# The order of weight splits, input squares and latent transposes around three block boundaries of a two-block transformer kernel

## The reference

```
f = swiglu(rms_norm(x, g[0]), w_in, w_out);  x = x + 0.5 * rms_norm(f, g[1])
h = rms_norm(x, g[2]);  m = attention(h);    x = x + rms_norm(m, g[3])
f = swiglu(rms_norm(x, g[4]), w_in, w_out);  x = x + 0.5 * rms_norm(f, g[5])
rms_norm(x, g) = x / sqrt(mean(x*x) + 1e-6) * g
```

## Time and profile before

| | |
|---|---|
| median of 3 runs | 1407.59 us (1407.07 to 1408.98) |
| the profiled execution, its own time | 1407.68 us |
| its span, first to last instruction | 1406.4 us |
| PE busy | 1378.2 us, 98% of the span |
| DVE busy | 918.6 us, 65% |
| ACT busy | 763.0 us, 54% |
| transfers | 297.19 MB, 211 GB/s on the mean |
| mean granted clock of TensorE | 0.999 |

### The profile page before, as it was taken

One profiled execution on the slowest core, in us unless ns is written; L12 is line 12 of the kernel. 1 busy time (PEld: TensorE's weight loads), 2 busy tenths in 40 slices (PEclk: granted clock), 3 DMA queues, 4 the chain that ended last, 5 costly groups with the idle time before them and its releaser, 6 DMA issues.

```text
span 1406.4 us, 18962 instructions
## 1 busy us (share of the span) xinstructions
PE 1378.2 (98%) x7530; PEld 1159.4 (82%) x7530; DVE 918.6 (65%) x1310; ACT 763.0 (54%) x1107; POOL 37.1 (3%) x72
## 2 busy tenths in 40 slices
PE   6999999999999999999999999999999999999998
PEld 5888799878888788888997888888888888788886
DVE  3667866777864866657576766657666477766653
ACT  4535456465454655546685554546555387654542
POOL 0000100000000000000241000000000000000000
PEclk9999999999999999999999999999999999999999
DMA  9756545558886588866434688866888651378872
GB/s 385 269 209 233 211 141 180 183 190 292 289 250 202 195 239 246 239 215 197 166 121 150 203 242 241 238 203 206 236 244 237 197 186 63 126 222 245 239 231 89
DMA packets 142233, 297.19 MB, mean 211 GB/s; under 512 B 65856, under 2 KB 80192, under 8 KB 138560
## 3 DMA queue, kind: packets, MB, share of 16 engines
q1 hardware_dynamic: 140128, 290.08, 64.6%
q10 hardware_dynamic: 2016, 5.90, 1.3%
HBM read 280.47 MB, written 15.47 MB: 210 GB/s over the span
## 4 chain that ended last, share of the span: by engine, by line
PE 90%; DVE 5%; ACT 3%; DMA 1%; issue 1%; SPq 0%; POOL 0%; ACTq 0%
PE PS L742 25%; PE PS L758 14%; PE PS L760 14%; PE PS L759 14%; PE PS L396 5%; PE PS L397 4%; PE PS L398 4%; DVE WL L1656 1%; PE PS L430 1%; DMA MC<-in_mod 1%; PE PS L431 1%; PE PS L432 1%; PE PS L979 1%; ACT WH L1080 1%; PE PS L728 1%
## 5 line engine op out<-in xcount | busy, mean ns | idle before, releaser
L1656 DVE TENSOR_TENSOR WL<-RAW,WH 128x1024 fp32r<-128x1024 f32 (+1 forms) x440 | 532.3, 1219 | 262.8 <-ACT WH L1080 262.1
L1080 ACT ACTIVATE WH<-RAW 128x1024 fp32r<-128x1024 f32 (+1 forms) x440 | 458.3, 1057 | 273.9 <-DMA RAW<-in_up 132.9
L758 PE MATMUL PS<-WH,XH 128*128 128x512 f32 (+1 forms) x928 | 363.9, 392 | 3.4 <-DVE XL L2127 2.9
L760 PE MATMUL PS<-WH,XL 128*128 128x512 f32 (+1 forms) x928 | 361.5, 389 | 0.0
L759 PE MATMUL PS<-WL,XH 128*128 128x512 f32 (+1 forms) x928 | 361.3, 389 | 0.0
L758 PEld LDWEIGHTS PS<-WH,XH 128*128 128x128 f32 x928 | 174.3, 188 | 42.9 <-DVE XL L2127 6.6
L760 PEld LDWEIGHTS PS<-WH,XL 128*128 128x128 f32 x928 | 174.3, 188 | 36.0
L759 PEld LDWEIGHTS PS<-WL,XH 128*128 128x128 f32 x928 | 174.4, 188 | 34.9
L742 PE MATMUL PS<-WH,GH 128*128 128x512 f32 x440 | 136.4, 391 | 0.0
L742 PE MATMUL PS<-WL,GH 128*128 128x512 f32 x440 | 135.7, 390 | 0.0
L742 PE MATMUL PS<-WH,GL 128*128 128x512 f32 x440 | 135.7, 390 | 0.0
(11 more groups left out here) (355 smaller groups left out, 1745.1 us busy)
## 6 DMA issues: line engine op xcount, KB each, us to landing
RAW<-in_up SPq DMA_DIRECT2D x220, 512.0 KB, 4.4
RAW<-in_down SPq DMA_DIRECT2D x110, 512.0 KB, 4.3
RAW<-in_win SPq DMA_DIRECT2D x28, 512.0 KB, 4.7
laid<-BT SPq DMA_DIRECT2D x55, 256.0 KB, 4.9
RG<-laid SPq DMA_DIRECT2D x55, 256.0 KB, 4.9
MC<-in_mod SPq DMA_DIRECT2D x8, 1024.0 KB, 11.5
RAW<-in_mod SPq DMA_DIRECT2D x8, 1024.0 KB, 5.7
RAW<-in_sbqk SPq DMA_DIRECT2D x16, 512.0 KB, 4.8
```

The source lines that it names most:

```text
L758: e.matmul(o_[:, 0:n], l, w[:, s], start=(k == 0), stop=False, skip_group_check=True)
L760: m = e.matmul(o_[:, 0:n], ll, w[:, s], start=False, stop=(k == KD - 1), skip_group_check=True)
L1080: e.activation(WH[s][:, 0:c], RAW[s][:, 0:c], ACT.Copy).then_inc(*sig("hi", j))
L1656: e.tensor_tensor(WL[s][:, 0:c], RAW[s][:, 0:c], WH[s][:, 0:c].bitcast(F32), ALU.subtract).then_inc(*sig("lo", j))
```

## The change

It touches the order of calls only; no operation is added, removed or resized.

- ACT, b = 1 and b = 6, row block 1: the split of c0+6 and the square of x for row block 0 move behind the two `turned` calls of row block 1; the split of c0+5 stays ahead of them. At b = 6, row block 0, the split of c0+3 joins that of c0+2, and that of c0+4 moves ahead of the second half.
- ACT, b = 5: the splits of c0+5 and c0+6 leave the boundary. After it, c0+5 (`mlakv` 1) is split behind `latents_turned(0)`, and c0+6 and c0+7 (`mlaq` 0 and 1) behind `latents(1)` and the table load, ahead of `keys_kept(0, 0)`; c0+8 and c0+9 follow later.
- DVE, b = 1 and b = 6: both halves are scaled and the first is made low before the split of c0+5, and the reciprocal of `scale_of_input(b, 0)` stands behind the second half. At b = 6 the split of c0+4 moves behind `renewed`, and that of c0+3 ahead of the low part of row block 0's second half. At b = 5 the splits of c0+4 to c0+6 leave the chain: c0+4 is split at the boundary's end, c0+5 ahead of `latents(1)`, c0+6 behind it and ahead of `latents_gained(1)`, and c0+7 behind `latents_low(1)`.
- PE: `latents_turned(0)` is run at p = 7 and not at p = 6, that is behind `mla_step(2, 1)`.

```diff
--- before.py
+++ after.py
@@ -1019,7 +1019,7 @@
                 if p == 3:
                     turn(5, 1, 0)
                     turn(5, 1, 1)
-                if p == 6:
+                if p == 7:
                     latents_turned(0)
                 if p >= 4:
                     mla_step(p - 4, 1)
@@ -1379,10 +1379,10 @@
                 square_of(b, 0, 1)
                 root(b, 0)
                 if b == 6:
-                    split(c0 + 2)
+                    split(c0 + 3)
                     turned(b, 0, 0)
+                    split(c0 + 4)
                     turned(b, 0, 1)
-                    split(c0 + 4)
                 elif b < 7:
                     split(c0 + 4)
                     turned(b, 0, 0)
@@ -1393,13 +1393,24 @@
                     turned(b, 0, 1)
                 square_of(b, 1, 1)
                 root(b, 1)
-                if b < 7:
+                if b in (1, 6):
+                    split(c0 + 5)
+                    turned(b, 1, 0)
+                    turned(b, 1, 1)
+                    split(c0 + 6)
+                    scale_of_input(b, 0)
+                    scale_of_input(b, 1)
+                elif b == 5:
+                    scale_of_input(b, 0)
+                    turned(b, 1, 0)
+                    turned(b, 1, 1)
+                    between()
+                    scale_of_input(b, 1)
+                elif b < 7:
                     split(c0 + 6)
                     scale_of_input(b, 0)
                     turned(b, 1, 0)
                     turned(b, 1, 1)
-                    if b == 5:
-                        between()
                     scale_of_input(b, 1)
                 ac.wait_ge(*at("x", b, 1, 1))
                 for n in {1: (3, 4)}.get(b, (b + 3,)):
@@ -1606,10 +1617,11 @@
                 latents(0)
 
             boundary(5, chunk["mla", 0], first_latents)
-            split(chunk["mlaq", 2])
             latents_turned(0)
+            split(chunk["mlakv", 1])
             latents(1)
             e.preload_act_table_set("exp_and_others")
+            split(chunk["mlaq", 1])
             keys_kept(0, 0)
             latents_turned(1)
             keys_kept(0, 1)
@@ -2181,8 +2193,8 @@
                     scaled(b, 0, 0)
                     turned(b, 0, 0)
                     scaled(b, 0, 1)
+                    split(c0 + 3)
                     turned(b, 0, 1)
-                    split(c0 + 3)
                 elif 1 < b < 6:
                     split(c0 + 3)
                     scaled(b, 0, 0)
@@ -2198,32 +2210,45 @@
                     turned(b, 0, 1)
                 added(b, 1)
                 sum_of(b, 1)
-                if b < 7:
+                if b < 5:
                     split(c0 + 4)
                 inverse(b, 1)
                 renewed(b, 1, 0)
                 renewed(b, 1, 1)
+                if b == 6:
+                    split(c0 + 4)
                 if b < 7:
-                    if b < 2:
+                    if b in (1, 6):
+                        scaled(b, 1, 0)
+                        scaled(b, 1, 1)
+                        turned(b, 1, 0)
+                        split(c0 + 5)
+                        turned(b, 1, 1)
+                        scale_of_input(b, 0)
+                    elif b == 5:
+                        scale_of_input(b, 0)
+                        scale_of_latents(0)
+                        scaled(b, 1, 0)
+                        scaled(b, 1, 1)
+                        turned(b, 1, 0)
+                        turned(b, 1, 1)
+                        between()
+                        split(c0 + 4)
+                    elif b < 2:
                         scaled(b, 1, 0)
                         split(c0 + 5)
                         turned(b, 1, 0)
-                        if b:
-                            scale_of_input(b, 0)
                         scaled(b, 1, 1)
                         turned(b, 1, 1)
                     else:
                         split(c0 + 5)
                         scale_of_input(b, 0)
-                        if b == 5:
-                            scale_of_latents(0)
                         scaled(b, 1, 0)
                         scaled(b, 1, 1)
                         turned(b, 1, 0)
                         turned(b, 1, 1)
-                    if b == 5:
-                        between()
-                    split(c0 + 6)
+                    if b != 5:
+                        split(c0 + 6)
                     if b:
                         scale_of_input(b, 1)
 
@@ -2432,10 +2457,12 @@
             scale_of_latents(1)
             latents_gained(0)
             latents_low(0)
-            split(chunk["mlaq", 1])
+            split(chunk["mlakv", 1])
             latents(1)
+            split(chunk["mlaq", 0])
             latents_gained(1)
             latents_low(1)
+            split(chunk["mlaq", 1])
             values_kept_of(0, 1)
             split(chunk["mlaq", 3])
             values_kept_of(1, 1)
```

## The result

The changed kernel takes 1414.05 us (median of 5 runs, 1409.88 to 1415.34), the kernel before, on the same chip, 1408.41 us (1407.07 to 1408.99). The ratio of the two is 1.004, with a 95% interval of 1.0029 to 1.005: 5.6 us slower. The forecast was 1409.6 and its range ended at 1412.0. The profiled execution took 1415.34 us against 1407.68, 7.66 more; it is the slowest of the five.

What follows compares the result with a forecast made beforehand. PE was taken to bound the kernel, so only its waits could change the time. The terms 0.45 + 0.25 + 1.3 = +2.0 us on 1407.68 gave 1409.7, with the median 0.09 lower, 1409.6 us; range 1406.8 to 1412.0.

Steps and rivals of the forecast that it cites:

- b = 1: Row block 1 starts 0.5 us earlier on PE, but c0+7 comes later and PE waits at step (7,0): +0.45 us.
- XL's wait: PE's wait at the head of row block 1: nearly 0 at b = 1 and 6, about 1.3 us at b = 5.
- step (7,0): PE's wait there for c0+7's low part grows to about 1.6 us at b = 1, about 1 us at b = 6.
- b = 6: XL comes 0.88 us earlier, but c0+7 is low only at 1234.2, so step (7,0) starts later: +0.25 us.
- b = 5 up to keys(1, 0): PE gains 0.56 us at XL, but two mlaq splits on ACT delay KR, CH and CL of row block 1: +1.3 us.
- that for CL: PE's wait at keys(1, 0) in b = 5 for row block 1's CL, claimed to be about 2.4 us.
- KR: At b = 5, ACT's KR of row block 1 comes 7.0 us behind row block 0's CH, 5.2 before.
- The sum of the waits: The terms of b = 1, b = 6 and b = 5 together: 0.45 + 0.25 + 1.3 = +2.0 us.
- rival (a): PE's clock falls behind the new 2.5 us wait at keys(1, 0): 2.1 us more, 1411.7 us; chance 0.08.
- (b): Moved work fits ACT's idle time at b = 1, 5 and 6, gains stay: -2.35 us, 1405.2 us; chance 0.08.
- (c): ACT's later work meets the scores, or DVE is late for step (6,0): 0.6 at two places, 1410.8; chance 0.14.
- (d): The edits cancel: each first wait shrinks by as much as the second grows: 1407.6 us; chance 0.10.

Runs made afterwards that it cites:

- e4: The changed kernel with nine extra 512-column matmuls that PE runs inside its wait for CL ahead of keys(1, 0): 1410.07 us, ratio 1.0015 to the kernel before.
- e10: The kernel before with one PE pause of 1.48 us in the middle of a feed-forward: 1410.29 us, ratio 1.0018.
- e8: The kernel before with one PE pause of 5.81 us in the middle of a feed-forward: 1417.07 us, ratio 1.0063.
- e2: The changed kernel with only its edits of b = 5, b = 1 and 6 as in the kernel before: 1412.20 us, ratio 1.0028.
- e5: The kernel before with three copies on ACT ahead of latents_turned(1), which lengthen the wait for CL: 1413.91 us, ratio 1.0040.
- e9: The changed kernel with ACT's moved work in its idle time and mlaq 0 and 1 split behind row block 1's latents: 1405.45 us, ratio 0.9984 to the kernel before.
- e6: The kernel before with one PE pause of 2.56 us in the middle of a feed-forward: 1411.90 us, ratio 1.0027.
- e7: The changed kernel with ACT's moved work put into ACT's idle time, mlaq 1 still ahead of latents_turned(1): 1407.45 us, ratio 0.9995 to the kernel before.
- e1: The changed kernel with only its edits of b = 1 and 6, b = 5 as in the kernel before: 1408.66 us, ratio 1.0006.
- e11: The changed kernel measured again, with no edit: 1413.35 us, ratio 1.0033 to the kernel before.
- e3: The changed kernel with mlaq 0 and 1 split behind latents_turned(1) on ACT and latents_low(1) on DVE: 1408.24 us, ratio 1.0004 to the kernel before.

## Why the prediction was wrong

- b = 1: right. Forecast +0.45, measured +0.59; the gain row issues took 1.02 us and not 0.82. XL's wait went, step (7,0) waits 1.53 for the forecast's 1.6, and ACT's second square is the cause as named.
- b = 6: right. +0.25, measured +0.24.
- b = 5 up to keys(1, 0): right, in each term. +1.3, measured +1.30. The wait for XL is 1.28 (forecast about 1.3), that for CL 2.32 (forecast about 2.4), KR comes 7.0 us behind CH.
- The sum of the waits that the reordering makes, +2.0, is what e4 measures with the clock kept (+2.2), and what the three fastest runs of the changed kernel show (1409.6 to 1410.2 for a forecast of 1409.6).
- The step that failed is rival (a), in chance and in price. The sum put the clock at nothing, because "the wait is only a third longer than one that did nothing", and (a) got 0.08. Ten of thirteen runs came out 1.5 to 5.9 us above the forecast, seven of them with a mean clock below that of all 73 runs on record of the kernel before. The comparison took one profiled execution for what always happens: behind the very wait that "did nothing", the 1.85 us for XL, the clock fell in the profiles of e10 and e8. (The 0.37 us that the text gives for a 448-column matmul there isn't in the earlier trace rows: the first one behind the wait has 0.47, the next ones 0.37.) The price of 2.1 us was half of the 4.2 us at the start of the span. That the lower level runs at half pace is right, but its length was mis-sized: about 10 us and 4.73 us lost in the changed kernel, about 7 and 3.1 in e2, 3.4 and 1.5 in e5.
- The trace of the kernel before had a second row that spoke for (a). At the end of the span, where PE's last matmul ends at 1400.08, the clock falls 2.6 us later, about as long an idle time as the 2.5 us forecast for keys(1, 0) (over all 13 profiles it is 2.0 to 5.3 us there):

```profile
1400.00:1402.70 2.70, 0.08 (x1) 0.00 (x0) 2.13 (x5) 1.67 (x5) 0.00 (x0) 1.00 0.00 0
1402.70:1406.40 3.70, 0.00 (x0) 0.00 (x0) 1.00 (x2) 0.00 (x0) 0.00 (x0) 0.50 0.35 142
```

- The Trainium skill, TensorE: Matmul & The Clock Gate, section "What's actually happening", says that the clock is throttled to half by default and that activity releases it. The runs agree: in e8, behind the pause of 5.81 us, the clock is 0.66 and 0.83 in the two windows, and in e4, where PE worked through the wait, it is 1.00. What a wait must be like for the fall is not settled by my runs.
- Rivals (b), (c) and (d) did not occur. The slack that (b) asked for was there only once ACT's work had been put into its gaps and the splits of `mlaq` behind the latents, in e9.

What stays open is why the clock falls behind a wait in one run and not in another of the same kernel. Other waits near by aren't needed (e6, e8, e10), nor is the place b = 5 (e6, e8). Whether they make the fall more likely, no run took apart.

## What to carry to other kernels

Work that is moved off a chain on an in-order engine has only moved behind it: find the next instruction of that engine for which the bound engine waits, and put the work into a gap of the engine rather than at its end. Where a reordering leaves a wait of 1.5 to 2.5 us on TensorE, count the clock as well, and look at more than one run: a spread of single times that the kernel before doesn't have (here 5.5 us against 2), with a lower mean clock in the long ones, is its sign. Cheap filler matmuls in an unavoidable wait keep the clock, and were worth some 3.4 us here (e4's +2.2 against the changed kernel's +5.6).

## What the runs showed of the hardware that was not expected

TensorE's lower level can come in mid-kernel behind a wait of 1.51 us (e7) or 1.85 us (e8, e10), and then holds while PE works: about 10 us in the changed kernel, with a granted clock of 0.50. Behind the 1.5 us at c0+7 (e1, the changed kernel) no profile shows it. Whether it comes differs from run to run of one kernel. It can come at the start as well, as in e11 behind a wait for data, after the clock had been full; the profiles of e3, e6, e7 and e9 have the same there.

```profile
15.81 1.19 PE L502 MATMUL PS<-MC,SILC 128*32 128x256 f32 x16 [2.44 <-DMA MC<-in_mod]
17.00:20.00 3.00, 3.00 (x16) 3.00 (x15) 1.22 (x1) 1.33 (x2) 0.00 (x0) 0.50 0.98 403
20.00:24.00 4.00, 4.00 (x41) 3.28 (x41) 1.29 (x4) 1.56 (x3) 0.00 (x0) 1.00 1.04 425
```

Beside it, the load of ACT's function table took 1.28 us in all 24 places of the kernel before, and in 17 of them the next activation started within 0.02 us of its end, for example 1147.68 to 1148.96 and 1148.97 at b = 5 of the kernel before.
